# A delta rule's log-decay sums by a DRAM row and one broadcast a round in place of eight matmuls, with its decay masks made at the round's beginning

## What is computed

```python
decay = jnp.cumsum(g, axis=-1)
diff = decay[..., :, None] - decay[..., None, :]
gamma = jnp.where(tril, jnp.exp(jnp.where(tril, diff, 0.0)), 0.0)
n_mat = jnp.where(strict, jnp.einsum('bhnid,bhnjd->bhnij', k_beta, k) * gamma, 0.0)
sol = lax.linalg.triangular_solve(eye + n_mat, rhs, left_side=True, lower=True, unit_diagonal=True)
qk = jnp.where(tril, jnp.einsum('bhnid,bhnjd->bhnij', q, k) * gamma, 0.0)
q_dec = q * jnp.exp(decay)[..., None]
```

## Time and profile before

| | |
|---|---|
| median of 3 runs | 2430.76 us (2428.01 to 2435.98) |
| profiled execution | 2432.12 us |
| its span, first to last instruction | 2430.3 us |
| granted TensorE clock, mean | 0.992 |
| PE busy | 2381.2 us, 98% |
| DVE busy | 1299.3 us, 53% |
| ACT busy | 809.8 us, 33% |
| POOL busy | 232.2 us, 10% |
| delta rounds | 118 to 600 us |

### The profile page before, as it was taken

One profiled execution on the slowest core, in us unless ns is written; L12 is line 12 of the kernel. 1 busy time (PEld: TensorE's weight loads), 2 busy tenths in 40 slices (PEclk: granted clock), 3 DMA queues, 4 the chain that ended last, 5 costly groups with the idle time before them and its releaser, 6 DMA issues.

```text
span 2430.3 us, 29514 instructions
## 1 busy us (share of the span) xinstructions
PE 2381.2 (98%) x11588; PEld 1979.7 (81%) x11588; DVE 1299.3 (53%) x1721; ACT 809.8 (33%) x1377; POOL 232.2 (10%) x161
## 2 busy tenths in 40 slices
PE   7999999999999999999999999999999999999998
PEld 6788888888787878988787788888888888888776
DVE  5675757574456557633385773334343344433755
ACT  4232333333443446522244432212221222322434
POOL 4010101011010100001140420000000000001400
PEclk9999999999999999999999999999999999999999
DMA  7632333343433424543221232333323332333222
GB/s 175 109 74 62 82 66 76 65 78 87 113 87 70 87 70 140 169 151 104 78 87 56 83 105 79 104 104 99 99 78 103 104 97 85 96 104 122 70 70 87
DMA packets 232876, 229.27 MB, mean 94 GB/s; under 512 B 18256, under 2 KB 226128, under 8 KB 232784
## 3 DMA queue, kind: packets, MB, share of 16 engines
q1 hardware_dynamic: 231584, 226.43, 34.2%
q10 hardware_dynamic: 1200, 1.57, 0.2%
HBM read 223.25 MB, written 4.72 MB: 94 GB/s over the span
## 4 chain that ended last, share of the span: by engine, by line
PE 88%; DVE 6%; issue 3%; ACT 1%; DMA 1%; POOL 0%; DVEq 0%; ACTq 0%; SPq 0%; POOLq 0%
PE acc L885 23%; PE acc L887 23%; PE acc L886 23%; PE acc L1212 2%; PE acc L1213 2%; PE acc L1217 2%; DVE weights_lo L1349 1%; PE m L1032 1%; DVE work L1830 1%; PE acc L1085 1%; PE acc L1087 1%; PE acc L1086 1%; PE m L964 1%; PE m L970 1%; PE m L1040 1%
## 5 line engine op out<-in xcount | busy, mean ns | idle before, releaser
L885 PE MATMUL acc<-input_hi,weights_hi 128*128 128x512 f32 (+1 forms) x2776 | 1092.3, 393 | 16.1 <-DVE weights_lo L1349 14.8
L887 PE MATMUL acc<-input_hi,weights_lo 128*128 128x512 f32 (+1 forms) x2776 | 1070.4, 386 | 0.0
L886 PE MATMUL acc<-input_lo,weights_hi 128*128 128x512 f32 (+1 forms) x2776 | 1069.6, 385 | 0.0
L1349 DVE TENSOR_TENSOR weights_lo<-weights_raw,weights_hi 128x1024 fp32r<-128x1024 f32 x400 | 538.2, 1360 | 312.8 <-ACT weights_hi L458 311.3
L885 PEld LDWEIGHTS acc<-input_hi,weights_hi 128*128 128x128 f32 x2776 | 523.7, 189 | 129.4 <-DVE weights_lo L1349 15.8
L458 ACT ACTIVATE weights_hi<-weights_raw 128x1024 fp32r<-128x1024 f32 x400 | 417.7, 1058 | 612.4 <-PE acc L887 562.8
L887 PEld LDWEIGHTS acc<-input_hi,weights_lo 128*128 128x128 f32 x2776 | 522.9, 188 | 105.4
L886 PEld LDWEIGHTS acc<-input_lo,weights_hi 128*128 128x128 f32 x2776 | 524.0, 189 | 99.5 <-issue 1.9
L2047 POOL TENSOR_TENSOR small<-small 128x4 f32<-128x4 f32 (+1 forms) x19 | 25.4, 1336 | 813.7 <-DVE small L1579 375.8
L1774 DVE COPY work<-acc 128x512 f32<-128x512 f32 x48 | 31.1, 684 | 126.5 <-PE acc L887 116.0
L2109 POOL TENSOR_TENSOR work<-work 128x512 f32<-128x512 f32 x42 | 54.4, 1294 | 335.6 <-ACT work L740 332.6
(11 more groups left out here) (285 smaller groups left out, 2199.0 us busy)
## 6 DMA issues: line engine op xcount, KB each, us to landing
weights_raw<-in_c_w_in SPq DMA_DIRECT2D x128, 512.0 KB, 3.8
weights_raw<-in_ab_w_in SPq DMA_DIRECT2D x126, 512.0 KB, 5.3
weights_raw<-in_m_w_kv SPq DMA_DIRECT2D x32, 512.0 KB, 3.5
weights_raw<-in_ab_w_out SPq DMA_DIRECT2D x32, 512.0 KB, 4.8
weights_raw<-in_m_w_q SPq DMA_DIRECT2D x32, 512.0 KB, 3.4
weights_raw<-in_c_w_out SPq DMA_DIRECT2D x32, 512.0 KB, 4.1
residual<-in_x SPq DMA_DIRECT2D x32, 256.0 KB, 5.9
weights_raw<-in_m_w_o SPq DMA_DIRECT2D x16, 512.0 KB, 3.6
```

The source lines that it names most:

```text
L885: pe.matmul(out, w_hi[:, o:o + P], hi(kt), start=kt == 0, stop=False)
L886: pe.matmul(out, w_hi[:, o:o + P], lo(kt), start=False, stop=False)
L887: last = pe.matmul(out, w_lo[:, o:o + P], hi(kt), start=False, stop=kt == last_kt)
L1349: TTO(w_lo[:, s * CW:(s + 1) * CW], raw[:, c * CW:(c + 1) * CW], w_hi[:, s * CW:(s + 1) * CW].bitcast(F32), ALU.subtract).then_inc(lo_read ...
```

## The change

The running sums are made once as rows. In round 0, before chunk 15, PE transposes `decay` (128 x 32) into m01, DVE copies the 32 x 128 result, and ACT sends it (16 KB) to a DRAM tensor `decays`. In each delta round SP, after it has loaded the first four chunks, fetches the 8 rows of the round's two heads as one 4 KB line broadcast to 128 partitions (512 KB) into `gam`. At the round's beginning ACT takes the Exp of it into the queries' place, and DVE subtracts the column sums and adds the mask. The 8 matmuls of the increments in `dk` and the copy of `pair_g` go; `dk` on PE waits for `q_eps`, not for `k_out`. `qd` goes behind `nt`. By `D_PLACES` the slots become tr 1, dk 3, qb 10, e1 14, vb 15, e2 17, e5 26, p4 28, and all later hops one slot earlier.

```diff
-D_PLACES = {"tr": 5, "dk": 6, "qb": 4, "e1": 1, "vb": 2, "e2": 8, "e5": 2, "p": 1, "y4": 3, "y5": 2, "uw": 2,
+D_PLACES = {"tr": 2, "dk": 7, "qb": 4, "e1": 1, "vb": 2, "e2": 9, "e5": 2, "p": 1, "y4": 3, "y5": 2, "uw": 2,
@@ SP, ab_loads
+                        if 1 <= like <= 4 and (j, c) == (1, 0):
+                            decay_rows(like - 1 + n)
+            def decay_rows(i):
+                sp.wait_ge(decay_out, 16)
+                sp.wait_ge(chunk_used, C_AB + 12 + 16 * i)
+                sp.dma_start(gam, dram["decays"].rearrange("(i r) n -> i (r n)", r=2 * TT)[bass.ds(i, 1), :].broadcast_to([P, 2 * T]))\
+                    .then_inc(decay_in, 16)
@@ ACT, delta: begin, tr, dk; ab_round of round 0
+                    act.wait_ge(decay_in, 16 * i + 16)
+                    act.activation(wq_q, tiles(gam), ACT.Exp).then_inc(*GA.did("edec"))
...
+                    act.wait_ge(decay_out, 16)
...
                     act.wait_ge(*GV("gam", i))
-                    act.activation(prod, flat(m01), ACT.Exp).then_inc(*GA.did("edec"))
                     act.activation(gam, gam, ACT.Exp).then_inc(*GA.did("gam"))
...
+                    if like == 0 and c == 15:
+                        act.wait_ge(*SV("decay_rows"))
+                        act.dma_start(dram["decays"], gate_buf[0:32, 0:P]).then_inc(decay_out, 16)
@@ PE, decay_rows (called before chunk 15 of round 0); delta: dk
+                pe.wait_ge(*SV("decay"))
+                pe.transpose(M[1][0:32, 0:P], decay, ident).then_inc(*SM.did("decay_rows"))
...
-                    pe.wait_ge(*GV("k_out", i))
+                    pe.wait_ge(*GV("q_eps", i))
                     for h, t in ht:
-                        pe.matmul(m(m01, h, t), pair_g[:, h * TT + t:h * TT + t + 1].broadcast_to([P, P]), c_("cumsum"),
-                                  start=True, stop=True)
                         last = pe.matmul(m(m23, h, t), kc[:, o(h, t)], kc[:, o(h, t)], start=True, stop=True)
@@ DVE, decay_rows (round 0, chunk 15); delta: begin, tr, dk
+                dve.wait_ge(*SM("decay_rows"))
+                dve.tensor_copy(gate_buf[0:32, 0:P], M[1][0:32, 0:P]).then_inc(*SV.did("decay_rows"))
...
-                if name == "tr":
+                if name == "begin":
                     GV.round(i)
-                    dve.tensor_copy(pair_g, g_col[:, hc]).then_inc(*GV.did())
+                    dve.wait_ge(*GA("edec", i))
+                    then(TTO(tiles(gam), tiles(gam), over_row(decay[:, hc], 8, P), ALU.subtract))
+                    TTO(tiles(gam), tiles(gam), over_tiles(c_("causal"), 8), ALU.add).then_inc(*GV.did("gam"))
...
-                    dve.wait_ge(*GM("dk", i))
-
-                    then(TTO(tiles(gam), psum_tiles(m01), over_row(decay[:, hc], 8, P), ALU.subtract))
-                    then(TTO(tiles(gam), tiles(gam), over_tiles(c_("causal"), 8), ALU.add), "gam")
-                    dve.wait_ge(*GA("edec", i))
-                    TTO(wq_q, tiles(qc), tiles(prod), ALU.mult).then_inc(*GV.did("qd"))
                     dve.wait_ge(*GA("gam", i))
                     then(TTO(tiles(gam), tiles(gam), over_row(k_inv, 8, P), ALU.mult))
+                    dve.wait_ge(*GM("dk", i))
                     TTO(n_t, flat(m23), gam, ALU.mult).then_inc(*GV.did("nt"))
+                    TTO(wq_q, wq_q, tiles(qc), ALU.mult).then_inc(*GV.did("qd"))
```

More of the change, by code:

```diff
@@ L227, in build @@
         t1, t2, t3, t4, t5 = (cols(32) for _ in range(5))
-        pair_g = cols(2 * TT)
         a_gain, b_gain, neg_lam, coef = (cols(1) for _ in range(4))
@@ L307, in build @@
         const_set = sem("const_set")
+        decay_out, decay_in = sem("decay_out"), sem("decay_in")
         SM, SA, SV, SG = steps("start_mm"), steps("start_act"), steps("start_vec"), steps("start_pool")
@@ L925, in decays, with decay_rows @@
                 last.then_inc(*SM.did("decays"))
+            def decay_rows():
+                pe.wait_ge(*SV("decay"))
+                pe.transpose(M[1][0:32, 0:P], decay, ident).then_inc(*SM.did("decay_rows"))
             def delta(name, i):
@@ L1062, in ab_round @@
                         decays()
+                    if like == 0 and c == 15:
+                        decay_rows()
                     j, kt0 = start_chunk(c) if like == 0 else (c // 4, 4 * (c % 4))
@@ L1456, in halve @@
                                            op=ALU.add, negate=True), tag)
-                if name == "tr":
+                if name == "begin":
                     GV.round(i)
-                    dve.tensor_copy(pair_g, g_col[:, hc]).then_inc(*GV.did())
+                    dve.wait_ge(*GA("edec", i))
+                    then(TTO(tiles(gam), tiles(gam), over_row(decay[:, hc], 8, P), ALU.subtract))
+                    TTO(tiles(gam), tiles(gam), over_tiles(c_("causal"), 8), ALU.add).then_inc(*GV.did("gam"))
+                elif name == "tr":
                     dve.wait_ge(*GM("tr", i))
-                    TS(q_eps, M[2][:, 0:8], EPS * HD, 4 * HD * EPS * EPS, ALU.mult, ALU.add).then_inc(*GV.did())
+                    TS(q_eps, M[2][:, 0:8], EPS * HD, 4 * HD * EPS * EPS, ALU.mult, ALU.add).then_inc(*GV.did("q_eps"))
                     dve.wait_ge(*GA("k_sq", i))
@@ L2180 @@
         dram["blocks"] = nc.dram_tensor("diagonal_blocks", (64, BASE * BASE), F32, kind="Internal").ap()
+        dram["decays"] = nc.dram_tensor("decay_rows", (4 * HEADS, P), F32, kind="Internal").ap()
         dram["inverses"] = nc.dram_tensor("block_inverses", (BASE, 64 * BASE), F32, kind="Internal").ap()
```

## The result

The change is slower by 6.2 us: a median of 2438.11 us (2434.41 to 2440.31, 8 runs) against 2431.88 (2428.01 to 2435.98, 8 runs) of the kernel before on the same chip, a ratio of 1.0025 with a 95% interval of 1.0017 to 1.0034. I had forecast 2428.1 us, within 2420.3 to 2434.0. So it lies 10 us off the forecast and above the range, though within 0.3% of the kernel before.

The account below looks back on a forecast made before the run. PE, busy 98% of the span, was taken as the bound: -7.2 - 2.5 - 0.4 + 0.2 + 7.2 = -2.7, so 2430.8 - 2.7 = 2428.1 us. The range was 2420.3 to 2434 us.

Parts of the forecast that it names:

- Half of `dk`'s passes, -7.2: On PE in `dk`: 16 passes of 0.112 us fewer a round, 7.2 us in four, counted in full.
- `vb`, +7.2: PE reaches `vb` before DVE's second gate ends and waits 1.8 us a round, 7.2 in four.
- both blockings by POOL: POOL's two products block DVE: 1.8 us on convolution products behind `qd`, then the second gate until POOL is done, +26.6.
- `tr`, -0.4: PE's wait at `tr` for ACT's squares goes, as the last hop comes one slot earlier: -0.4 us.
- the transpose, +0.2: One additional PE transpose in round 0, at least twice the pass distance: 0.2 us.
- The fetch, nothing: First delta round's broadcast: `dk` waits if landing exceeds 5.2 us; sum cost taken as 0, with 1.6 for the range.
- `vb` free: Rival: DVE runs ahead by 1.8 us or more, so `vb` does not wait: -9.9, 2420.9 us; chance 0.30.
- a slow round trip: Rival: first delta round's DRAM fetch is late, holding `dk`; a 20 us fetch gives 2441.5 us; chance 0.04.
- DVE later still: Rival: `vb` waits 4.3 us a round or more on DVE; 4.5 gives 2438.9 us; chance 0.04.
- the forecast's own range: 2424.5 to 2433.5 us, from `vb` waits of 0.9 to 2.8, fetch +1.6, state steps 1 either way, before stretching.
- The state steps keep their distances; they shift by a slot against DVE's convolutions, and I take 0, with 1 us either way.: PE's waits in the delta rounds' state steps stay unchanged: 0, with 1 us either way.
- So the wait at `p4` goes: -2.5.: PE's wait at `p4` for `t16`, in two rounds, vanishes as the solve ends near 3 us earlier: -2.5 us.

Follow-up runs that it names:

- experiment 1: The change with the slot table of the kernel before (dk 6, qb 12, vb 17, p4 29, uw 36): 2422.68 us, ratio 0.9961 to the kernel before.
- experiment 4: The change with one more wait on POOL, so its second mask product starts only after the values' second gate: 2432.34 us, ratio 1.0001.
- experiment 8: The kernel before plus a 512 KB broadcast fetch a round, data unused, at the change's place in SP's program: 2431.89 us, ratio 1.0000.
- experiment 3: The change with `uw` back at slot 36 and all hops behind it one slot later: 2434.55 us, ratio 1.0009 to the kernel before.
- experiment 7: The kernel before with the slot table of the change and nothing else: 2473.31 us, ratio 1.0169 to the kernel before.
- experiment 5: The change with `dk` at slot 4 instead of 3, behind the split of chunk 19, later slots kept: 2430.16 us, ratio 0.9994.
- experiment 2: The change with `vb` at slot 17 instead of 15 and nothing else moved: 2431.69 us, ratio 0.9997 to the kernel before.
- experiment 6: The change with `p4` and all hops behind it one slot later in the last delta round alone: 2432.12 us, ratio 1.0003.
- experiment 9: The change with `dk` at 4, `vb` at 17, `uw` at 36, the rest of its table kept: 2422.87 us, ratio 0.9961.

## Why the prediction was wrong

**What held.** *Half of `dk`'s passes, -7.2*: experiment 1 is 9.8 us faster than before with the arithmetic alone, of which 2.5 are the wait at `p4`. *`vb`, +7.2*: measured +6.6, 1.81 in the first round against 1.8 forecast. The steps of that sum held too: from the start of `tr` at 120.24, `qk` ends at +24.25 (forecast +24.1) and the gate at +27.24 (+27.2), and both blockings by POOL came where they were put; experiment 4 shows the second to be the cause. *`tr`, -0.4*, and *the transpose, +0.2* (0.1). *The fetch, nothing*: 3.5 us in the first round, under the 5.2 from which it would have cost; experiment 8 finds no price either, within its 2 us and without the late start of the first round. The range of landings was low, though: up to 9.7 against the 8.1 of the earlier trace rows. The rivals (`vb` free, a slow round trip, DVE later still) all fell. Two small slips in the forecast's figures change nothing: the `vb`-free case is 2420.9 in the rivals and 2420.3 in the range, and +4.0 and +1.6 end the forecast's own range at 2433.7, not at 2433.5.

**What failed, first: "The state steps keep their distances; they shift by a slot against DVE's convolutions, and I take 0, with 1 us either way."** They cost +3.1. I looked at distances on PE and at DVE's convolutions, and not at where the splits stand on ACT. One slot put `uw` ahead of the split of chunk 27. Experiment 3 takes the term back, and experiment 7 shows it in the kernel before.

**What failed, second: "So the wait at `p4` goes: -2.5."** Two rounds had it. In the first it went, in the last it grew from 1.5 to 3.2, so the term is +0.7 in place of -2.5. The sum saw that SP sends the blocks only behind the load of chunk 23, and left it at the delay of issue. It took the landing times as they were. The solve's end did come 2.3 us earlier, against the 3 forecast, although the blocks' way had grown from 4.8 to 8.6 us. But the inverses' write landed in 7.8 us instead of 5.1, and took the gain back. That a transfer takes longer behind a load was not in the sum. Experiment 5 moves the load of chunk 23 off the blocks, the whole row of transfers behind it comes earlier, and the wait goes. That it is the place in the queue behind the loads which delays a write, and not a busy memory, is argued and not shown: block writes issued 0.4 us behind a load took 4.5 to 6.9 us, and the inverses land within 0.7 to 1.7 us of the last load ahead of them in the change, in the kernel before and in experiments 1, 2, 5, 6 and 9; no run separates the two.

**What was not in it at all: the clock, +2.9.** I counted a wait at its own length. Behind the 3.2 us at `p4` the granted clock was near half till about 535.7. Experiment 6 shortens this wait to 1.9 and the clock stays. The link rests on one profiled execution of each kernel.

Together: the forecast had -2.7 against the profiled execution. With 3.1 for the state steps, 3.2 for `p4`, 2.9 for the clock, -0.6 for `vb` and -0.1 for the transpose it is +5.8, and the spans show +6.0. My range took in 1 us either way for the state steps and nothing for the clock, and so ended 4 us too low. That the time is still within 0.3% of before is no merit of the sum: three losses that it left out stand against a gain that it had right.

## What to carry to other kernels

A table of slots moves more than its own engine: for each hop that changes its slot, list what it changes places with in the program order of every other engine and DMA queue (here a split on ACT, and a 512 KB load on SP), even where the distances stay. Price an earlier hop against the chain that feeds it: where PE waits for the answer anyway, an earlier slot gains nothing, and a wait may cost its own length again in clock. And try a change of arithmetic with the old table first; here it was worth 9.8 us, and the new table gave 15.4 back.

## What the runs showed of the hardware

The granted clock fell to half in waits of PE of 3.2 us (the change), 5.3 (experiment 2) and 5.7 (experiment 4) and stayed there behind them, and did not behind 1.5 (before) and 1.9 (experiment 6). It was not a matter of the wait's length alone: behind 3.3 us in experiment 3 `p4` took 2.48 us, where it takes 2.0 at full clock and 3.75 in the change, and the windows show 0.80 and 0.77. Nor does it take a wait: in experiment 1 the clock was 0.62 in the 4 us from 360, and in experiment 3 0.61 in the 4 us from 244, both just behind `tr` and with PE busy for all but 0.2 us of the 4 us ahead.

Eight writes of 8 KB, issued 0.4 us behind a load of 512 KB on the same queue, landed in 4.5 to 6.9 us in the last delta round (median 5.3; over all four rounds 1.5 to 6.9, median 3.0); 9 us behind it, in 1.4 to 1.5 (over all four 1.4 to 2.1, median 1.5). Loads in this stretch took 7.3 to 11.8 us in both kernels, so a fetch or a write has neighbours that a row of another stretch doesn't show.

An instruction of DVE as small as 64 x 8 took 1.91 us beside POOL's product (experiment 4), against 0.16 in the changed kernel: its size is no protection.
